# Early modulation blocks of a two-layer diffusion backbone: their loads, their sums and the score steps placed elsewhere

## What is computed

```python
def reference(...):
    for l in range(DEPTH):                                   # 2
        sh1, sc1, g1, sh2, sc2, g2 = split(silu(c) @ mod_w[l] + mod_b[l])       # modulation, latent
        ch1, cs1, cg1, ch2, cs2, cg2 = split(silu(c_ctx) @ mod_w[l] + mod_b[l])  # modulation, context
        hx = rms_norm(x_lat) * (1 + sc1) + sh1               # the same for context
        # layer 0: neighbourhood attention (8 heads) beside retention (8 heads); layer 1: windowed attention
        x_lat = x_lat + g1 * yx
        hx2 = rms_norm(x_lat) * (1 + sc2) + sh2
        x_lat = x_lat + g2 * peer(hx2, peer_w_q[l], peer_sub_keys[l], peer_u[l], peer_v[l])
        # the context stream goes the same way in layer 0, and is not needed after layer 1

def peer(h, w_q, sub_keys, u, v):                            # 8 heads, 128 + 128 keys, 16 experts each
    s = scores of h @ w_q against the sub keys; top 16 of each half, top 16 of their 256 sums
    return sum over 128 experts of gate * gelu(h . u[expert]) * v[expert]        # per token
```

## Time and profile before

| | us |
|---|---|
| median of 3 runs (lowest, highest) | 2695.13 (2683.86, 2700.23) |
| the profiled execution, its own time | 2718.0 |
| span of the profiled execution, first to last instruction | 2716.2 |
| early part, up to the first gather | 331.5 |
| first gather to first v gather | 83.3 |
| busy: PE, DVE, POOL, ACT | 1902.1, 1733.5, 1709.4, 384.7 |
| DMA moved | 959.07 MB, mean 353 GB/s |

### The profile page before, as it was taken

One profiled execution on the slowest core, in us unless ns is written; L12 is line 12 of the kernel. 1 busy time (PEld: TensorE's weight loads), 2 busy tenths in 40 slices (PEclk: granted clock), 3 DMA queues, 4 the chain that ended last, 5 costly groups with the idle time before them and its releaser, 6 DMA issues.

```text
span 2716.2 us, 23064 instructions
## 1 busy us (share of the span) xinstructions
PE 1902.1 (70%) x7218; PEld 813.2 (30%) x7218; DVE 1733.5 (64%) x4290; ACT 384.7 (14%) x793; POOL 1709.4 (63%) x1575
## 2 busy tenths in 40 slices
PE   6999965887786885666565665678737886566556
PEld 2446652222343341222111211224532442222111
DVE  2633597675788776676655667653597966666641
ACT  1021111101222120101010111111111210101100
POOL 1100146767677777777777777773157777777775
PEclk8967987998888997888777867789868988877769
DMA  7774498999999999999999999996599999999998
GB/s 265 260 244 140 141 322 305 406 406 406 388 384 344 371 399 406 406 396 372 408 406 406 377 374 406 351 405 245 194 326 380 396 379 401 406 406 400 373 373 351
DMA packets 312521, 959.07 MB, mean 353 GB/s; under 512 B 30144, under 2 KB 65104, under 8 KB 312016
## 3 DMA queue, kind: packets, MB, share of 16 engines
q0 software_dynamic: 225792, 822.18, 78.3%
q1 hardware_dynamic: 82448, 127.47, 13.5%
q10 hardware_dynamic: 4160, 7.95, 0.8%
HBM read 956.43 MB, written 1.05 MB: 353 GB/s over the span
## 4 chain that ended last, share of the span: by engine, by line
POOL 30%; PE 23%; DMA 20%; DVE 14%; issue 12%; ACT 1%; SPq 0%; POOLq 0%; ACTq 0%; DVEq 0%
POOL u_rows L499 14%; POOL v_rows L499 14%; DMA v_rows<-in_peer_v,idx_turned 14%; PE ps L1000 8%; DVE u_rows L1893 5%; PE ps L669 3%; DMA u_rows<-in_peer_u,idx 3%; PE ps L914 1%; DMA wring<-in_ab_w_in 1%; PE ps L567 1%; PE ps L975 1%; PE ps L556 1%; POOL resid L499 1%; DMA u_rows<-in_peer_v,idx_turned 1%; PE ps L709 1%
## 5 line engine op out<-in xcount | busy, mean ns | idle before, releaser
L1893 DVE CUSTOM_DVE_ANT_0 u_rows<-u_rows,h 128x1024 f32<-128x1024 f32 x768 | 930.7, 1224 | 510.6 <-DMA u_rows<-in_peer_u,idx 500.6
L1000 PE MATMUL ps<-v_rows,spread_w 128*32 128x512 f32 x2636 | 838.1, 761 | 524.5 <-DMA v_rows<-in_peer_v,idx_turned 484.9
L499 POOL DMA_INDIRECT u_rows<-in_peer_u,idx x768 | 842.5, 1097 | 449.6 <-issue 220.4
L499 POOL DMA_INDIRECT v_rows<-in_peer_v,idx_turned x659 | 728.9, 1106 | 259.1 <-issue 177.1
L1000 PEld LDWEIGHTS ps<-v_rows,spread_w 128*32 128x32 f32 x2636 | 165.6, 126 | 1052.7 <-issue 1035.1
L669 PE MATMUL ps<-wring,arena 128*128 128x512 f32 x528 | 251.5, 623 | 20.7 <-DVE arena L1402 8.4
L975 PE MATMUL ps<-arena,wring 128*128 128x256 f32 (+1 forms) x1024 | 201.9, 358 | 2.7 <-ACT arena L1228 2.7
L975 PEld LDWEIGHTS ps<-arena,wring 128*128 128x128 f32 x1024 | 174.9, 216 | 54.6 <-issue 37.6
L537 POOL DMA_DIRECT2D u_rows<-in_mod_w x20 | 14.7, 735 | 217.9 <-DVE v_rows L1371 166.7
L669 PEld LDWEIGHTS ps<-wring,arena 128*128 128x128 f32 x528 | 99.6, 198 | 173.2 <-issue 140.3
L556 PE MATMUL ps<-table,arena 128*128 128x128 f32 x432 | 84.4, 324 | 75.4 <-ACT arena L1053 33.4
(11 more groups left out here) (232 smaller groups left out, 2008.1 us busy)
## 6 DMA issues: line engine op xcount, KB each, us to landing
wring<-in_mod_w SPq DMA_DIRECT2D x64, 512.0 KB, 5.8
...
```

The lines of the kernel that those rows point to most:

```text
L499: nc.gpsimd.indirect_dma_start(out=rows, out_offset=None, in_=table, in_offset=bass.IndirectOffsetOnAxis(ap=index, axis=0)).then_inc(lande ...
L1000: mm = nc.tensor.matmul(PS[32 * q:32 * q + 32, 6 + e, :], spread_w[:, s // PAIR % 2, 32 * c:32 * c + 32], v_buffer(v_place(x)[0])[:, e * 5 ...
L1893: nc.vector.tensor_tensor_reduce(UB[:, slot % NU, :], UB[:, slot % NU, :], H2[:, g // 8 % 3, :], 1.0, 0.0, ALU.mult, ALU.add, av_[:, 0, g ...
```

## The change

- POOL's first five early loads wait for `pr_half` 1, 2, 3, 4 and 5, one each; before, all five waited for 1.
- `EM_ADD` puts 1, 2, 1, 2, ... adds behind the first 16 steps of `proj(0)` and 2 behind the rest: 44 adds instead of 52. `outp(0)` has 2, 1, 2, ... behind its 13 steps: 20 instead of 12.
- `EM_SUM`: five block sums in `proj(0)` instead of six, two in `outp(0)`, and the eighth behind PE's ten first steps of `prep(0)`. So `early_mod` comes as blocks 0 to 4 and 5 to 7, and block 5 goes to bank 7 with 6 and 7.
- PE's wait for `em_ev` 1 (the columns of bank 5 have been read) stood ahead of the first matmul of `attn(0)`; now it stands ahead of item 1's last matmuls, the first that write bank 5.
- In window 0 the 12 score steps are spread over slots 1 to 68 instead of 1 to 34, the latent pass over 68 to 232 instead of 34 to 232.

```diff
         def early_cols(i0, i1):
-            return PS[:, 5 if i0 < 6 else 7, 128 + 4 * i0:128 + 4 * i1]
+            return PS[:, 5 if i0 < 5 else 7, 128 + 4 * i0:128 + 4 * i1]
...
-        BESIDE = {0: table_of((c_prep(0)[READY[0]:], 1, 34), (c1[:-12], 34, 14 * TOPK + 8),
+        BESIDE = {0: table_of((c_prep(0)[READY[0]:], 1, 4 * TOPK + 4), (c1[:-12], 4 * TOPK + 4, 14 * TOPK + 8),
...
-        EM_ADD = [{s: 2 for s in range(26)}, {s: 1 for s in range(12)}]
-        EM_SUM = [{4 * i + 5: 1 for i in range(6)}, {6: 1, 12: 1}]
+        EM_ADD = [{s: 1 + s % 2 if s < 16 else 2 for s in range(26)}, {s: 2 - s % 2 for s in range(13)}]
+        EM_SUM = [{8: 1, 13: 1, 18: 1, 22: 1, 25: 1}, {5: 1, 10: 1}]
...
-            pool.wait_ge(pr_half, 1)
             for n in range(32):
-                if n >= NE:
+                if n < NE:
+                    pool.wait_ge(pr_half, n + 1)
+                else:
                     pool.wait_ge(em_sum, 2 * (n - NE + 1))
...
-                    if i == 6:
+                    if i == 5:
                         pe.wait_ge(row_ev, ROW[0, "g2"] + 1)
...
-                if n == 0:
-                    pe.wait_ge(em_ev, 1)
...
+                        if m == 1:
+                            pe.wait_ge(em_ev, 1)
...
             rest = ready(0, prep(0))
+            next(sums_)
...
-            early_mod(0, 6)
+            early_mod(0, 5)
```

4 lines of the change are left out of this document (2 added, 2 removed).

## The result

The changed kernel takes 2734.09 us (median of 4; 2727.74 to 2753.16), the kernel before in the same comparison 2697.68 us (median of 4). The ratio is 1.0125, 95% interval 1.0077 to 1.0172: 21 to 46 us slower. I had predicted 2704 us with a range of 2680 to 2722, so the time lies outside it, on the slow side.

What follows compares the result with a forecast made beforehand. The prediction took the stream of gathers as the main bound, with DVE the bound in places. Its terms, 7.8 + 2.3 + 3.6 - 15.6 + 11 = +9.1 us, gave 2725.3 profiled, 2704 us as median, range 2680 to 2722.

Steps and rivals of the forecast that it cites:

- Term 1: proj(0): staggered loads make PE wait twice, less what unit 2, sparser adds and attn(0) win; +7.8 us.
- both waits: proj(0), end of units 3 and 4: PE waits 7.2 and 5.4 us for DVE's work behind late adds.
- Unit 2's slow stretch: proj(0): half unit of 5.28 us instead of 3.55 at lower clock; expected gone with one or two loads in flight.
- Term 2: outp(0): 20 adds instead of 12, three of 0.75 us in PE's way at the norms; +2.3 us (0 to 3).
- The five pieces still to load have DMA to themselves: outp(0): the early loads left to make were taken to share DMA with nothing.
- Term 3: First gather: POOL waits for the eighth block sum, now behind the fifth w_q step; +3.6 us (0 to 4.5).
- Term 4: Slots 0 to 36: fewer score steps ahead of the first v gather, DMA full sooner; -15.6 us (-8 to -19).
- nothing is kept, because DMA's bytes are the same: Rival on slots 0 to 36: the gain is lost again, sum +25, 2720 us; 0.19 together with slower latent pass.
- Term 5: Latent pass, 164 slots instead of 198: DVE's need reaches 99% of DMA's; +11 us (0 to +25).
- 3 for the norm: Latent pass: 3 us of the +11, since its norm now stops DVE and PE with DMA full.
- the latent pass makes it slower than before: Rival: DVE becomes the bound from attention to output projection, +21 to +25 there, 2716 us; 0.19 together with nothing kept.
- a few us of waits inside the pass: Latent pass: enough, with DVE at 99%, to push its need past DMA's 2.71 us a slot.

Runs made afterwards that it cites:

- e8: e2 with the first five early loads again all waiting for the first half unit alone; 2701.57 us, ratio 0.9999.
- e1: Kernel before with only the new slots: score steps over 1 to 68, latent pass over 68 to 232; 2717.46 us, ratio 1.0066.
- e2: Changed kernel with its old table of slots (score steps over 1 to 34), so only the early part differs from before; 2715.74 us, ratio 1.0032.
- e11: e8 with score steps over slots 1 to 50, latent pass 50 to 232, PE's steps one slot later, last block sum ending outp(0); 2677.48 us, ratio 0.9902.
- e13: Kernel before with only PE's wait ahead of attn(0) moved to its second product with v; 2684.26 us, ratio 0.9955.
- e6: e1 with half of each dot product of slots 128 to 247 left out; 2716.41 us in one run, no ratio.
- e7: Kernel before with half of each dot product of slots 128 to 247 left out; 2683.01 us in one run, no ratio.
- e5: e1 with PE's steps beside the first window's gathers one slot later, DVE's and ACT's unmoved; ratio 0.9973.
- e9: Kernel before, old table of slots, with PE's steps of the first window one slot later; 2702.03 us, ratio 0.9989.

## Why the prediction was wrong

**Term 1, `proj(0)`, +7.8: right.** 155.9 became 163.5, +7.6, with both waits within 0.7 us of the forecast. Its halves don't come out as cleanly. By my terms the staggered loads cost 16.0 and win 4.0 in unit 2, net 12.0; by e8 they cost 17.0 net. The rest of the gain was 4.2 by my terms and is 9.2 by e8 (6.9 against e1). Unit 2's slow stretch is gone in e8, with the five loads at once, so it was not theirs alone, and I had left out a third stand of 1.68 us. That the sum is right within 0.2 us is in part luck.

**Term 2, `outp(0)`, +2.3: too small.** It is +6.3 (38.8 to 45.1 us, the same in e2 and e8). "The five pieces still to load have DMA to themselves" failed: `w_out` pieces were on their way too, and PE waited 1.53 us for one. The two adds ahead of the second norm were forecast, at 1.5 us. But PE stands 3.87 us there instead of 0.85 and turns the rows behind it at the lower clock (granted 0.65 from 313 to 317 us), 3.44 us instead of 2.05, which I had put at nothing.

**Term 3, the first gather, +3.6: near.** +4.4, released by PE's sum as forecast; e11 shows that the sum can stand in `outp(0)` for less.

**What terms 1 to 3 left out.** At full clock they come to 21 us (e2 against e1), 7 more than my 13.7. The ratio of e2 shows only 9 (1 to 16). The wait that the change takes from the head of `attn(0)`, for which I put 1.0 us, is worth about 12 alone (e13, 3 to 21). I had read the 79.3 us of this stretch in the one profile that I had as the kernel's own, though its clock stood at 0.50 there.

**Term 4, slots 0 to 36, -15.6: right in kind, too large.** First gather to slot 64: -23.6 in the two profiles compared, -20.1 in e1, and the first v gather after 73.1 us (forecast 72.5). That looks like more than forecast. But my -15.6 was meant as time won for good, after five weight pieces, 6.5 us, are moved behind it. Eight pieces are, with 4.7 MB less in all, about 12 us, and what is won for good is 8 or 9 us. So the rival "nothing is kept, because DMA's bytes are the same" holds for more than half of the 20 us.

**Term 5, the latent pass, +11 (0 to +25): the step that decided.** Measured +39 (e1: 593.9 against 554.4), of which some 15 are the bytes of term 4 coming back and some 25 lost time. The step that failed is the mechanism, not only a size: I divided DVE's work by its slots, found 99% of DMA's need, and priced the pass by what DVE would lack. By e6 and e7 DVE's load in slots 128 to 248 is worth 13 to 16 us in both tables and explains 3 of their 26.4 us of difference there. What the dense table does, by the waits of e1 and e5, is to bring the steps of the pass closer together than the chain PE, DVE, ACT, PE inside one attention step takes. PE stands at the step, in order, in front of v matmuls that are ready; v buffers come free late; POOL's one queue stops; DMA is no longer full. One slot more (e5) takes 22 of the 25 us of lost time away. The "3 for the norm" is 11: I had seen that it now stops DVE and PE with DMA full, and priced only DVE's share. The 13 us that e5 is still behind the old table lie between slots 128 and 176 (156.0 us against 142.0), and they are bytes: 383 GB/s over 156 us against 360 over 142, 8.6 MB more, which would take 21 us at 404 GB/s. Against the old table with the same shift (e9) 21.3 us are left, half of them lost time; that half stays open. The 16% idle that I gave for DVE outside the retention is that of the whole stretch; outside it is 21% (138.9 of 175 us busy).

The rival "the latent pass makes it slower than before" had the right place and the right sign, but DVE's load as its mechanism, and a price of 21 to 25. Its own condition, "a few us of waits inside the pass", was in the profile before: PE already stood 11.0 us in front of exps and POOL 42.1 us in front of v buffers between slots 64 and 248.

**The sum.** Forecast +9.1: 13.7 - 15.6 + 11. By the traces at full clock: 21 - 20 + 39 = +40; with the moved bytes taken out of both, 21 - 8 + 25 = +38. By the ratios: +34 and +37 for the whole, +18 for the table, +9 for the early part.
